# A decoder layer on one core: in the attention stage's merge products, high and low rows of the input side by side in one product of 512 columns, the halves added by VectorE

## The reference, cut to what matters

```python
h = rms_norm(x, g_attn)
proj = h @ w_in
q_n, kv_n, gate_n, qkv_f, f_logit, merge_logit = jnp.split(proj, [S1, S2, S3, S4, S5], axis=-1)
...
merge = jax.nn.sigmoid(merge_logit + b_merge).reshape(B, T, 2, D_MODEL)
y = merge[:, :, 0] * (o_nsa @ w_up_nsa) + merge[:, :, 1] * (o_fox @ w_up_fox)
x = x + y @ w_out
x = x + moe_ffn(rms_norm(x, g_mlp), w_router, b_router, w_e_gate, b_e_gate, w_e_up, b_e_up, w_e_down, b_e_down)
```

## Time and profile before

| | us |
|---|---|
| median of 3 runs | 1135.39 (1135.31 to 1137.51) |
| the profiled execution | 1134.49 |
| its span, first to last instruction | 1132.6 |
| TensorE busy | 1062.2 (94%) |
| VectorE busy | 451.0 (40%) |
| ScalarE busy | 170.8 (15%) |
| GpSimd busy | 90.4 (8%) |
| granted TensorE clock, mean | 0.998 |
| DMA, mean rate | 389 GB/s |

### The profile page before, as it was taken

The page is one execution under the profiler, slowest core; times in us unless marked ns, Lnnn a source line. Parts: engine busy times, 40 slices in busy tenths (PEclk is TensorE's granted clock), DMA queues, the critical chain, the costliest instruction groups (busy, mean ns, idle before and its releaser), DMA issues.

```text
span 1132.6 us, 14582 instructions
## 1 busy us (share of the span) xinstructions
PE 1062.2 (94%) x5719; PEld 508.4 (45%) x5719; DVE 451.0 (40%) x1070; ACT 170.8 (15%) x342; POOL 90.4 (8%) x89
## 2 busy tenths in 40 slices
PE   9999999999999998998888899998889888899987
PEld 7779899843333333333333333333333333333323
DVE  5883666533333343233333332323333333333333
ACT  7546655300000000000000000000000000000000
POOL 3227446000000000000000000000000000000000
PEclk9999999999999999999999999999999999999999
DMA  9836424999999999999999999999999999999996
GB/s 381 360 149 251 196 76 174 422 422 430 425 428 428 428 427 428 429 429 428 428 428 429 429 427 428 428 426 428 429 426 428 429 428 428 430 428 428 428 424 276
DMA packets 34592, 440.09 MB, mean 389 GB/s; under 512 B 3793, under 2 KB 5202, under 8 KB 6898
## 3 DMA queue, kind: packets, MB, share of 16 engines
q1 hardware_dynamic: 33808, 438.71, 91.7%
q10 hardware_dynamic: 738, 0.73, 0.2%
HBM read 438.38 MB, written 1.05 MB: 388 GB/s over the span
## 4 chain that ended last, share of the span: by engine, by line
DMA 50%; PE 48%; ACT 1%; issue 1%; DVE 1%; SPq 0%; POOL 0%; DVEq 0%; ACTq 0%; POOLq 0%
PE bank L1899 25%; DMA ring<-in_w_e_up_dram 24%; DMA ring<-in_w_e_gate_dram 21%; DMA ring<-in_w_e_down_dram 3%; PE bank L1870 2%; DMA ring<-in_w_fk_dram 2%; PE bank L1660 1%; PE bank L1661 1%; PE bank L1662 1%; PE bank L1886 1%; PE bank L1505 1%; PE bank L1943 1%; PE bank L1747 1%; PE bank L1706 1%; PE bank L1748 1%; PE bank L1749 1%
## 5 line engine op out<-in xcount | busy, mean ns | idle before, releaser
L1899 PE MATMUL bank<-ring,heads 128*64 128x512 f32 x3004 | 677.2, 597 | 21.4 <-DMA ring<-in_w_e_gate_dram 17.8
L1899 PEld LDWEIGHTS bank<-ring,heads 128*64 128x64 f32 x3004 | 202.5, 136 | 416.7 <-issue 360.3
L1443 DVE TENSOR_TENSOR x<-x,bank 128x512 f32<-128x512 f32 x124 | 79.7, 684 | 123.2 <-PE bank L1923 123.2
L891 ACT ACTIVATE y_hi<-bank,small 128x512 fp32r<-128x512 f32 x31 | 21.3, 687 | 692.2 <-PE bank L1899 692.2
L1413 DVE SCALAR_TENSOR_TENSOR y_lo<-bank,small,y_hi 128x512 fp32r<-128x512 f32 x31 | 23.2, 750 | 174.9 <-ACT y_hi L891 174.9
L698 POOL TENSOR_TENSOR x<-x,heads 128x256 f32<-128x256 f32 x2 | 1.4, 727 | 910.0 <-ACT heads L919 910.0
L405 POOL TENSOR_TENSOR w_lo<-ring,w_hi 128x1024 fp32r<-128x1024 f32 (+1 forms) x35 | 65.4, 1891 | 53.6 <-ACT w_hi L721 53.6
L1886 PE MATMUL bank<-bias_parts,e_sel 128*128 128x512 f32 x63 | 31.2, 494 | 38.2 <-DMA ring<-in_w_e_gate_dram 18.2
L721 ACT ACTIVATE w_hi<-ring 128x512 fp32r<-128x512 f32 (+2 forms) x82 | 57.1, 731 | 23.1 <-PE bank L1749 7.3
L1870 PE MATMUL bank<-work,xn 128*128 128x128 f32 x480 | 58.5, 275 | 0.0
L1419 DVE COPY heads<-bank 128x512 f32<-128x512 f32 x31 | 21.4, 691 | 93.0 <-PE bank L1943 93.0
(11 more groups left out here) (315 smaller groups left out, 1030.5 us busy)
## 6 DMA issues: line engine op xcount, KB each, us to landing
ring<-in_w_e_gate_dram SPq DMA_DIRECT2D x61, 2048.0 KB, 33.4
ring<-in_w_e_up_dram SPq DMA_DIRECT2D x61, 2048.0 KB, 35.0
ring<-in_w_e_down_dram SPq DMA_DIRECT2D x58, 2048.0 KB, 34.7
ring<-in_w_e_down_dram SPq DMA_DIRECT2D x12, 1024.0 KB, 27.9
ring<-in_w_merge_dram SPq DMA_DIRECT2D x4, 2048.0 KB, 8.0
spare<-in_w_e_gate_dram SPq DMA_DIRECT2D x2, 2048.0 KB, 15.0
ring<-in_w_out_dram SPq DMA_DIRECT2D x2, 2048.0 KB, 7.9
ring<-in_w_e_up_dram SPq DMA_DIRECT2D x4, 1024.0 KB, 8.3
```

What stands on the lines that cost most here:

```text
L1443: ins = nc.vector.tensor_tensor(x[:, t, 512 * h:512 * h + 512], x[:, t, 512 * h:512 * h + 512], bank67[:, j % 2, :], ALU.add)
L1899: last = mm(bank[C * half:C * half + C, :], lhs(kk), kept_row[half] if kept else w[:, k, 512 * half:512 * half + 512], start=(kk == 0 and ...
```

## The change

The high and low rows of the normed input lie side by side in one tile (`hT_both`), chunk by chunk, 256 and 256 columns. The high part of a weight chunk multiplies both in one product of 512 columns, so that high x high goes into the left half of the bank and high x low into the right; low x high is added to the right half by a product of 256 columns. VectorE then adds the two halves (`sum_merge`, a reduction over two elements) and writes the sum into `mergeT`, and ScalarE takes the tanh there in place. The bank is free for the next merge but one when the sum is made, not when the tanh is.

```diff
@@ -104,7 +104,8 @@
-            hT_hi, hT_lo = (parts.enter_context(nc.sbuf_tensor(n, [P, KD, T], F32R)) for n in ("hT_hi", "hT_lo"))
+            hT_both = parts.enter_context(nc.sbuf_tensor("hT_both", [P, KD, 2, T], F32R))
+            hT_hi, hT_lo = hT_both[:, :, 0, :], hT_both[:, :, 1, :]
@@ -823,8 +824,8 @@
             def keep_merge(c):

-                act.wait_ge(merge_done, c + 1)
-                nc.scalar.activation(mergeT[:, c, :], PJ[c % 2][:, 0:T], ACT.Tanh, scale=0.5,
+                act.wait_ge(merge_summed, c + 1)
+                nc.scalar.activation(mergeT[:, c, :], mergeT[:, c, :], ACT.Tanh, scale=0.5,
                                      bias=scaled[:, c:c + 1]).then_inc(merge_made, 1)
@@ -1162,7 +1163,16 @@
             keep_unit(11)
+
+            def sum_merge(c):
+
+                dve.wait_ge(merge_done, c + 1)
+                nc.vector.tensor_reduce(mergeT[:, c, :], PJ[c % 2][:, :].rearrange("p (h t) -> p t h", h=2), AX.X, ALU.add).then_inc(merge_summed, 1)
+            sum_merge(0)
+            sum_merge(1)
             keep_unit(13)
+            sum_merge(2)
+            sum_merge(3)
@@ -1216,6 +1226,7 @@
                 if i < PAIRS:
                     scale_p(i)
+                    sum_merge(EARLY + i)
@@ -1650,16 +1661,15 @@
                     if c >= 2:
-                        pe.wait_ge(merge_made, c - 1)
+                        pe.wait_ge(merge_summed, c - 1)
...
                 for k in ks:
-                    mm(PJ[c % 2][:, 0:T], w_hi[:, k, w], hT_hi[:, k, :], start=(k == 0), stop=False)
-                    mm(PJ[c % 2][:, 0:T], w_hi[:, k, w], hT_lo[:, k, :], start=False, stop=False)
-                    last = mm(PJ[c % 2][:, 0:T], w_lo[:, k, w], hT_hi[:, k, :], start=False, stop=(k == KD - 1))
+                    mm(PJ[c % 2][:, :], w_hi[:, k, w], hT_both[:, k, :, :].rearrange("p h t -> p (h t)"), start=(k == 0), stop=False)
+                    last = mm(PJ[c % 2][:, T:2 * T], w_lo[:, k, w], hT_hi[:, k, :], start=False, stop=(k == KD - 1))
@@ -1756,10 +1766,10 @@
-            pe.wait_ge(merge_made, 15)
+            pe.wait_ge(merge_summed, 15)
             lift(0, 0)
             turn_p(PAIRS - 1)
-            pe.wait_ge(merge_made, 16)
+            pe.wait_ge(merge_summed, 16)
             lift(1, 0)
```

More of the change, by code:

```diff
@@ L284, in build @@
             "s_done", "s_max", "p_made", "p_scaled", "p_turned", "pT_made", "o_done"))
-        merge_done, merge_made = sem("merge_done"), sem("merge_made")
+        merge_done, merge_made, merge_summed = sem("merge_done"), sem("merge_made"), sem("merge_summed")
         oT_hi_made, oT_lo_made, up_done, y_made, yT_hi_made, yT_lo_made, out_used, out_done = map(sem, (
```

## The result

The changed kernel takes 1140.91 us (median of 6 runs, 1139.77 to 1141.74) beside 1135.68 for the kernel before, timed together with it: +5.2 us, ratio 1.0044 with a 95% interval of 1.0034 to 1.0054. It is slower, as forecast, but by twice the forecast 2.6 us. The profiled execution took 1139.89 us (span 1138.0), so 5.4 more than that of before.

The account below looks back on a forecast made before the run. TensorE was taken to bound the merges and pairs, the expert weight load the end. The 5.51 us ring outlasts TensorE's 5.26, delaying that load by 2.6 us: 1135.39 becomes 1138.0, slower; range 1135.0 to 1141.2.

Parts of the forecast that it names:

- TensorE's gain: Merges: a wide product for two narrow ones takes 0.0134 us less per chunk, 0.107 per merge, 1.72 us for 128 chunks.
- the walk: Step-by-step start times from exponentials 0 at 102.62 us to the high part of lift piece 2 at 168.51, 2.63 late.
- the ring: Pair loop: exponentials, scaling, sum, tanh, high part, next exponentials wait in turn; 5.51 us in pairs 0 to 7, TensorE's pair 5.26.
- The sum: VectorE's added reduction per merge, 512 columns from PSUM: 0.68 us, bounds 0.416 and 1.283.
- the tanh: ScalarE's tanh, now reading the sums in SBUF: 0.49 us, bounds 0.40 and 0.50; it was 474 ns from PSUM.
- the rival of a dear sum: VectorE's sum costs 0.9 us, giving +5.2 and 1140.6; at the bound 1145.2; chance 0.15.
- the scaling: VectorE's scaling in each pair, a term of the ring: 1.40 us, and 1.16 from pair 8 on.
- The mask step: Ahead of pair 8 the causal mask is rewritten; its exponentials start 1.99 us after that rewrite starts, at 147.22.
- From the high part to the load: Lift piece 2's high part, GpSimd's low parts, fourth lift, expert weight load: no slack, all some 2.6 us later.
- The rival of a delay partly given back: Hops or high parts 0.1 us shorter per turn, so the ring yields 1.2 us less: +1.4, 1136.8; chance 0.24.

## Why the prediction was right in sign and half in size

- **TensorE's gain** was oversized: 0.055 us per pair, not 0.107. In merges 0 to 3, of which the walk counts 4 x 0.107 = 0.43, it was 0.29: from first to last product merges 0 and 1 take 5.72 for 5.81 us, merges 2 and 3 5.52 for 5.72. So 0.14 of the delay was missed here (exponentials 0 stand 0.42 apart in the two traces all the same, which is within the scatter of their starts); the rest of the gain is off the path in the changed kernel. From both, an estimate is 0.29 + 12 x 0.055 = 0.95 us for a kernel without the ring; the runs show 0.3 to 1.2, none of them told apart from zero.
- **The sum** at 0.68 and **the tanh** at 0.49 (0.51) were right, and the rival of a dear sum is out, though its 1140.6 is near the measured time: the sum costs what was said.
- **The ring** was right: 5.51 us for pair 0, 5.49 to 5.52 up to pair 7 once GpSimd is kept away, and cutting it takes the loss to zero.
- **The mis-sized term** is the scaling, "scaling 1.40" and "from pair 8 the scaling takes 1.16". That was its time with GpSimd idle. In the changed kernel the high part ends right ahead of the exponentials and GpSimd starts 0.18 us behind their start, for 2.38 us; the scaling begins 2.10 us behind it (108.14 to 110.24). So 0.43 to 0.46 us of the scaling lie under GpSimd in pairs 1 to 8, 0.6 in pairs 10 and 11, none in pairs 0 and 9, and lengthen it by 0.22 to 0.48. By starts of exponentials: pair 0 to 7 took 142.57 − 102.63 = 39.94 for 38.57, +1.37; 7 to 8 took 0.29 less than forecast; 8 to 9 +0.26; 9 to 10 nothing; 10 to 11 +0.46; from there to the high part +0.45. Together +2.25, and 2.63 + 2.25 is the measured 4.89 but for rounding.
- **The mask step**, "1.99 later", was too long and hid part of the miss. In the kernel before the first maxima of pair 8 stood 0.75 us idle behind the mask. The profile names the mask, long done, so it was most likely the scores, which TensorE was still making. In the changed kernel the scores were under way before the mask was even begun, and the maxima came right behind it. TensorE and VectorE before, then both after:

```profile
143.22 0.60 PE L1696 MATMUL bank<-heads 65*128 65x256 f32 x2
143.95 0.29 DVE L1174 CUSTOM_DVE_ANT_0 work<-bank,causal 128x128 f32<-128x128 f32 x1 [0.75 <-DVE causal L1208]
...
144.40 0.60 PE L1706 MATMUL bank<-heads 65*128 65x256 f32 x2
146.83 0.28 DVE L1218 TENSOR_SCALAR causal<-causal 128x256 f32<-128x256 f32 x1
147.14 0.29 DVE L1184 CUSTOM_DVE_ANT_0 work<-bank,causal 128x128 f32<-128x128 f32 x1
```

  The step took 148.31 − 146.83 = 1.48, 0.51 less than the walk has, while the longer scaling of pair 7 put 0.24 on.
- **From the high part to the load** the shift was passed on whole (4.89, 4.84, 4.85), as forecast. TensorE waited for GpSimd 0.98 us at the third lift, which the prediction didn't have, and 0.82 at the fourth. Its waits at the values of a pair were 3.4 us in seven, the longest 1.6.
- The rival of a delay partly given back went the wrong way round: no turn of the ring was shorter than its sum by more than 0.02 us, and only the mask step gave something back.
- The median sat 1.0 us above the profiled execution, for which 0.9 was allowed.
- That the stated range, up to 1141.2, holds the measured 1140.9 is luck: its upper part was there for a dear sum, which didn't come, and what came in its place was no term of the prediction.

## What to carry to other kernels

An added instruction on an engine with idle time need not cost anything by its length (the sum that nobody waited for didn't), but it can close a ring: follow it from the engine that waits for it back to itself, add the terms up, and compare with the pitch of the bounding engine. Then lay the other engines' instructions over the new times, since a duration read where VectorE and GpSimd didn't meet doesn't hold where they do. A consumer that may come one turn later, as the tanh here, can cut the ring without a cost of its own.

## What the runs showed of the hardware that I had not expected

- A VectorE product of two SBUF operands that starts during a GpSimd subtraction in SBUF ends only behind it, 0.14 to 0.29 us later: 2.61 us for a 128x256 that takes 0.48 alone, four of them together 3.53 for 1.41; 3.40 for 1.16 for the plain product. The rewrite of the mask, with one SBUF operand, is held too: 2.10 and 2.32 us for 0.28, both ending 0.15 behind GpSimd.
- It works in the other direction: GpSimd's 128x1024 piece takes 2.40 us alone, 2.46 to 2.48 when it starts among the products with about 0.2 us of one left, and 2.65 when it starts with 0.39 us of the last product left.
- Not held: the reciprocal of 4 columns (0.18 us at 110.03, beside GpSimd), and what reads PSUM: with GpSimd held back its 2.4 us lie beside sum and maxima, and the sum takes its 0.68 us; the low part of the attention output, from a bank and SBUF, takes 1.29 us beside GpSimd in the changed kernel (154.48) and 1.28 without it.
- Two products of 256 columns made into one of 512 save some 13 ns per chunk by the fk rows, and 6 or 13 ns in merges that run without a break (0.353 or 0.347 us for 0.360).
